# Mixture of experts: weights as whole float32 in column halves, in place of split parts, with a ring of twelve units

## The chip, the cores and the metric

One Trainium2 chip; the kernel runs on one NeuronCore. The metric is device time in microseconds of one execution, median of the runs.

## What is computed

Two network blocks over 256 tokens of width 1024. The first block is a retention and convolution mixer followed by a mixture of 32 experts, the second a gated MLP and a dilated attention. The change is in the experts only:

```
t = u.reshape(256, 1024)
# router: one of 4 groups, the 2 best of its 8 experts, weights -> combine (256 x 32)
for e in range(32):
    h = silu(t @ w_exp_gate[e]) * (t @ w_exp_up[e])          # 1024 x 512 each
    y = y + combine[:, e:e + 1] * (h @ w_exp_down[e])        # 512 x 1024
```

All of it is float32. An expert has three matrices of 2 MB, 32 experts 192 MB: half of what the kernel reads.

## The kernel before

**Units and ring.** Weights arrive in units of 1 MB, 128 partitions x 2048 numbers (`UC` = 4 chunks of 512 columns). An expert has six: gate 0 and 1, up 0 and 1 (each half of the 1024 inputs), down 0 and 1. During the experts the ring has six units of SBUF, one for each part (`SLOT_OF`). The SP queue issues all weight transfers in an order written out by hand (`expert_stream`, L635); each waits until TensorE has finished with the unit that lay in the slot before (`unit_done`).

**Split parts.** TensorE multiplies in the single-pass float32 format `fp32r`, whose operands are rounded. So that nothing is lost, every weight unit is split: ScalarE copies it rounded into `w_hi` (L2767), VectorE subtracts that from the unit and leaves the rest in `w_lo` over the unit itself (L2001; GpSimd does a quarter of the down part, L2373). Each product is made with both parts. Inputs are split as well, into two times 64 columns side by side (`xs`, `hs`): one weight load of 128 columns holds the rounded and the remaining part of 64 gathered tokens, and the two halves of the output are added later by a product with `fold` (L1193).

**One expert (`expert` on each engine, 64 slots of gathered tokens).** On TensorE in this order: two up units (8 chunks x 2 parts = 16 matmuls of 512 columns, L1132 and L1135), the gather of the next expert's tokens (48 bf16 matmuls of 64 columns: `h` in three bf16 parts times the selection `sel`, L1146), the scatter of the expert before (8 matmuls, L1154 and L1156), two transposes of the weighted selection (L1185), the fold (8 products, L1193), the next expert's gate units (16 matmuls), the down units (16 matmuls, L1124). ScalarE also empties PSUM (L2817, L2783), makes the slot weights (L2823), silu (L2825) and the rounded outputs `ye_hi` (L2803); VectorE makes `selT` (L2028), the product of gate and up (L2030), `hs` (L2032), `sel` (L1988) and `selw` (L1994) of experts ahead and `ye_lo` (L2013).

**Around the experts.** The gate units of expert 0 are loaded early into `first_gate`, rounded by ScalarE (L2730) and split by VectorE (L1817) while the mixer ends; up 0, gate 1 and down 0 are loaded into the ring at 531 to 537 us. The router runs from about 542 to 570 us. After expert 31, `scatter_whole` (L1165) adds its output; then VectorE adds the experts to the residual and the second block begins with four units that were loaded ahead (`units_ahead`, L684), the first two rounded by ScalarE (`hi_ahead`, L2798).

**Whole float32 elsewhere.** The ada and tail units of the mixer (`row_unit`, L827) are multiplied unsplit, as float32, in four column quarters of the array (32 columns each); spreads of 128 columns (L843) are float32 too. A float32 matmul stands in the trace as two records, an fp32r or bf16 one as one record.

Of the kernel before, what the change touches and what calls it, by code (L numbers as in the profile page):

```python
# [14 lines left out]
P = 128  # L15
T = 256
# [33 lines left out]
SLOT_OF = {"up": 0, "gate": 2, "down": 4}  # L50
# [48 lines left out]
def build(nc, a, out):  # L99
    with ExitStack() as ctx:  # L100
# [149 lines left out]

        slots_of, fills = [], []
        for n in range(len(units)):
            slots_of.append(n % RING2 if n < n_before else (n - n_before) % RING if n < first["a"] else (n - first["a"]) % RING2)
            fills.append(slots_of.count(slots_of[n]) - (n >= first["a"] and slots_of[n] in (SLOT_OF["gate"], SLOT_OF["gate"] + 1)))


        fills_before = [slots_of[:n_before].count(k) for k in range(RING)]
# [174 lines left out]
        def heads_T(t, tt):  # L432
# [61 lines left out]
        xs = single_pass("xs", KC, P, on=free0 + 3072)  # L494
        sel = nc.alloc_sbuf_tensor_at("sel", [P, NT, SLOTS], BF16, offset=ARENA_AT + 4 * (free0 + 4096))
        selw, _ = carve(NT, 2, SLOTS, on=free0 + 5120)
        selT = single_pass("selT", T, on=free0 + 5376)
        fold, _ = carve(SLOTS, on=free0 + 5632)
        slot_weight, _ = carve(2, on=free0 + 5696)
        weighted, _ = carve(T, on=free0 + 5700)  # L500
        hs = single_pass("hs", FF // P, P, on=free0 + 7424)
        gate_act, _ = carve(T, on=free0 + 7936)
        gate_out, _ = carve(FF, on=free0 + 8192)
        up_out, _ = carve(FF, on=free0 + 8704)
        ye_hi = single_pass("ye_hi", D, on=free0 + 9216)
        ye_lo = single_pass("ye_lo", D, on=free0 + 10240)
        ye, _ = carve(D, on=free0 + 9216)
        w_hi = [single_pass("w_hi_%d" % p, UC, W, on=on) for p, on in enumerate(
            (o_kc, o_vc, o_v, o_v + 2048, o_vc + 2048, o_XT))]
        w_lo = single_pass("w_lo", RING, UC, W)  # L510
# [7 lines left out]
        first_gate = [arena[:, o_:o_ + UC * W].rearrange("p (k c) -> p k c", k=UC) for o_ in (o_qT, o_kT)]  # L518
        first_lo = [single_pass("first_lo%d" % j, UC, W, on=on) for j, on in enumerate((o_qT, o_kT))]
# [27 lines left out]
        def order(kind, e, j, tail=False):  # L547

            return 2 + e * 6 + ({"up": 0, "gate_next": 2, "down": 2 if tail else 4}[kind] + j + 1)
# [6 lines left out]
        def _(sp):  # L556
# [34 lines left out]
            for n in range(n_before):  # L591
# [15 lines left out]
                if n == at_unit["conv", 1, 1]:  # L607

                    sp.wait_ge(S("unit_done"), end_of("ret", 1, 4))
                    for j in range(2):  # L610
                        sp.dma_start(first_gate[j].rearrange("p k c -> p (k c)"), moe_src("gate", 0, j)).then_inc(S("first_full"), 16)
# [2433 lines left out]
```

## Time and profile before

| | before |
|---|---|
| device time, median of 3 runs | 1739.13 us (1737.48 to 1742.75) |
| the profiled execution's own time | 1742.08 us |
| its span | 1740.3 us |
| TensorE busy | 1604.2 us (92%) |
| VectorE busy | 1214.6 us (70%) |
| ScalarE busy | 988.0 us (57%) |
| GpSimd busy | 473.1 us (27%) |
| read from HBM | 378.95 MB, 218 GB/s over the span |

How to read it: the shares are means over stages with different limits. The experts take the stretch from about 575 us (first gate product) to 1146 us (last scatter), a third of the span and more than half of the bytes. The granted TensorE clock is given as a share of full speed.

### The profile page before, as it was taken

Reading aid. Unit: us, or ns where it says so; the run is one execution under the profiler, and the core shown is the slowest. Engines: PE = TensorE matmul, PEld = TensorE weight load, DVE = VectorE, ACT = ScalarE, POOL = GpSimd, SP = SyncE. Lnnn points to the kernel's source line nnn. Section 1 sums busy time; section 2 is a strip of 40 time slices with the busy share of each in tenths; the row PEclk is TensorE's granted clock in tenths of the full one; section 3 lists DMA queues with packets and bytes.
Section 4 is the critical chain, followed back from the end, with each engine's and each line's share of the span. In section 5 each row is a group of like instructions: output and inputs, shape, how many; then the busy total and the mean of one; then the engine's idle time right before and its main releaser. Section 6 shows DMA issues by size and latency. Waiting matters only on the chain.

```text
span 1740.3 us, 23452 instructions
## 1 busy us (share of the span) xinstructions
PE 1604.2 (92%) x8954; PEld 1291.7 (74%) x8954; DVE 1214.6 (70%) x1566; ACT 988.0 (57%) x1081; POOL 473.1 (27%) x132
## 2 busy tenths in 40 slices
PE   5999999999986889999999999969898899999986
PEld 2888888886664677778777878758787687878765
DVE  2688886765347899999999999972611863436793
ACT  2423245543434679898889898835344345464651
POOL 0000000110000031212121212128676476645562
PEclk9999999999996799999999999989999899999997
DMA  8623244246785489999989999837544453433430
GB/s 316 193 99 97 78 142 146 98 156 233 251 294 209 171 351 358 366 367 366 364 348 361 366 373 365 333 108 249 179 152 164 143 170 122 135 130 123 137 118 24
DMA packets 120869, 380.99 MB, mean 219 GB/s; under 512 B 9302, under 2 KB 11134, under 8 KB 96222
## 3 DMA queue, kind: packets, MB, share of 16 engines
q1 hardware_dynamic: 120798, 380.02, 60.0%
q8 instruction: 47, 0.77, 0.2%
q14 instruction: 24, 0.20, 0.0%
HBM read 378.95 MB, written 1.05 MB: 218 GB/s over the span
## 4 chain that ended last, share of the span: by engine, by line
PE 55%; DVE 20%; DMA 10%; issue 8%; ACT 6%; SPq 1%; DVEq 0%; POOL 0%; ACTq 0%; POOLq 0%
PE ps L743 10%; PE ps L744 9%; PE ps L750 9%; DVE w_lo L2001 6%; DMA ring<-in_w_exp_gate 5%; PE ps L908 3%; PE ps L907 3%; PE ps L914 3%; PE ps L1135 2%; PE ps L1132 2%; ACT w_hi L2767 2%; PE ps L807 1%; DVE arena L2263 1%; DVE arena L2265 1%; DMA ring<-in_w_exp_down 1%
## 5 line engine op out<-in xcount | busy, mean ns | idle before, releaser
L2469 ACT ACTIVATE w_hi<-ring 128x2048 fp32r<-128x2048 f32 x130 | 246.9, 1912 | 329.9 <-PE ps L750 141.7
L2001 DVE TENSOR_TENSOR w_lo<-ring,w_hi 128x2048 fp32r<-128x2048 f32 (+1 forms) x190 | 392.2, 2103 | 4.5 <-ACT w_hi L2767 4.5
L2394 POOL TENSOR_TENSOR w_lo<-ring,w_hi 128x2048 fp32r<-128x2048 f32 x71 | 334.1, 4727 | 189.5 <-ACT w_hi L2469 189.5
L2767 ACT ACTIVATE w_hi<-ring 128x2048 fp32r<-128x2048 f32 x190 | 364.9, 1922 | 15.5 <-DMA ring<-in_w_exp_gate 10.1
L2373 POOL TENSOR_TENSOR w_lo<-ring,w_hi 128x1024 fp32r<-128x1024 f32 x32 | 106.4, 3323 | 480.9 <-ACT w_hi L2767 480.9
L743 PE MATMUL ps<-w_hi,xt_hi 128*128 128x512 f32 x512 | 204.5, 399 | 7.2 <-ACT w_hi L2469 4.7
L1460 DVE TENSOR_TENSOR w_lo<-ring,w_hi 128x2048 fp32r<-128x2048 f32 x59 | 134.8, 2287 | 99.4 <-ACT w_hi L2469 99.0
L744 PE MATMUL ps<-w_hi,xt_lo 128*128 128x512 f32 x480 | 189.5, 395 | 0.0
L1132 PE MATMUL ps<-w_hi,xs 128*128 128x512 f32 x512 | 146.3, 408 | 9.0 <-DVE xs L2006 6.9
L743 PE MATMUL ps<-w_hi,yt_hi 128*128 128x512 f32 x352 | 141.1, 401 | 5.8 <-DVE yt_lo L1453 2.8
L1135 PE MATMUL ps<-w_lo,xs 128*128 128x512 f32 x504 | 141.2, 402 | 1.8
L750 PE MATMUL ps<-w_lo,xt_hi 128*128 128x512 f32 x512 | 126.8, 390 | 0.1
L743 PEld LDWEIGHTS ps<-w_hi,xt_hi 128*128 128x128 f32 x512 | 97.7, 191 | 32.6 <-ACT w_hi L2469 5.2
L1132 PEld LDWEIGHTS ps<-w_hi,xs 128*128 128x128 f32 x512 | 95.8, 192 | 32.5 <-issue 7.7
L1135 PEld LDWEIGHTS ps<-w_lo,xs 128*128 128x128 f32 x504 | 91.9, 190 | 35.8 <-DVE w_lo L2001 17.3
L750 PEld LDWEIGHTS ps<-w_lo,xt_hi 128*128 128x128 f32 x512 | 96.1, 188 | 20.6 <-POOL w_lo L2394 0.5
L744 PEld LDWEIGHTS ps<-w_hi,xt_lo 128*128 128x128 f32 x480 | 91.8, 191 | 18.9
L2400 POOL TENSOR_SCALAR arena<-arena 128x4 f32<-128x4 f32 x4 | 8.6, 2152 | 355.7 <-DVE arena L1660 355.7
L1552 DVE SCALAR_TENSOR_TENSOR arena<-arena 128x256 f32<-128x256 f32 x240 | 96.4, 482 | 0.0
L744 PE MATMUL ps<-w_hi,ut_lo_lat 128*128 128x512 f32 x224 | 88.3, 394 | 0.0
L743 PEld LDWEIGHTS ps<-w_hi,yt_hi 128*128 128x128 f32 x352 | 68.0, 193 | 26.7 <-issue 10.7
L750 PE MATMUL ps<-w_lo,yt_hi 128*128 128x512 f32 x352 | 87.1, 389 | 0.0
(330 smaller groups left out, 2904.4 us busy)
## 6 DMA issues: line engine op xcount, KB each, us to landing
ring<-in_w_exp_up SPq DMA_DIRECT2D x64, 1024.0 KB, 8.9
ring<-in_w_exp_down SPq DMA_DIRECT2D x64, 1024.0 KB, 8.0
ring<-in_w_exp_gate SPq DMA_DIRECT2D x62, 1024.0 KB, 6.3
ring<-in_w_in SPq DMA_DIRECT2D x40, 1024.0 KB, 5.1
ring<-in_b_w_in SPq DMA_DIRECT2D x40, 1024.0 KB, 5.1
ring<-in_w_ada SPq DMA_DIRECT2D x24, 1024.0 KB, 6.9
ring<-in_a_w_in SPq DMA_DIRECT2D x24, 1024.0 KB, 6.5
ring<-in_w_ret_out SPq DMA_DIRECT2D x8, 1024.0 KB, 5.4
```

The costliest lines, as they stand in the source:

```text
L743: pe.matmul(o[:, tt, :], hi[:, k, x_], w[:, c, :], start=(bias is None and j == 0 and c == 0), stop=False)
L744: pe.matmul(o[:, tt, :], lo[:, k, x_], w[:, c, :], start=False, stop=False)
L750: mm = pe.matmul(o[:, tt, :], hi[:, (UC * j + c + at) % (UC * nk), x_], w_lo2[:, slots_of[n], c, :], start=False, stop=(j == nk - 1 and c ...
L1132: pe.matmul(ps[:, bank, :], parts(c), w_hi[p][:, c, :], start=(begin and c == 0), stop=False)
L1135: mm = pe.matmul(ps[:, bank, :], parts(c), w_lo[:, p, c, :] if lo is None else lo[:, c, :], start=False, stop=(end and c == UC - 1))
L1460: dve.tensor_tensor(w_lo2[:, slots_of[n]], ring[:, slots_of[n]], w[:, :, :].bitcast(F32), ALU.subtract).then_inc(S("w_lo_vector"), 1)
L1552: ins = dve.scalar_tensor_tensor(conv[:, k, :], z, cwT[:, k, j:j + 1], conv[:, k, :], ALU.mult, ALU.add)
L2001: dve.tensor_tensor(w_lo[:, p, 0:upto], ring[:, p, 0:upto], w_hi[p][:, 0:upto, :].bitcast(F32), ALU.subtract).then_inc(S("lo_ready"), 1)
L2373: pool.tensor_tensor(w_lo[:, p, c:UC], ring[:, p, c:UC], w_hi[p][:, c:UC, :].bitcast(F32), ALU.subtract).then_inc(S("pool_lo"), 1)
L2394: pool.tensor_tensor(w_lo2[:, slots_of[n]], ring[:, slots_of[n]], w[:, :, :].bitcast(F32), ALU.subtract).then_inc(S("w_lo_full"), 1)
L2469: act.activation(part_of(n)[1][:, :, :], ring[:, slots_of[n]], ACT.Copy).then_inc(S("w_hi_full"), 1)
L2767: act.activation(w_hi[p][:, :, :], ring[:, p], ACT.Copy).then_inc(S("hi_ready"), 1)
```

## The change

Expert weights are no longer split. Each unit is multiplied as it lies, as whole float32, with 64 columns of inputs in the array instead of 128: gate and up (`gate_up_product`) run side by side, gate in columns 0 to 63 and up in columns 64 to 127 of the array, each with its own moving weights, and leave in one PSUM bank. The down product does the same with its two output halves. There are no `w_hi`, `w_lo`, `xs`, `hs` and `fold` any more, and no part of GpSimd in the experts. The space of `w_hi` becomes six more ring slots (`homes`), so that two experts' units fit (even experts in `ring`, odd ones in `homes`). Selections and gathers are made for two experts at once: 128 columns a matmul, half of the 1024 features after each expert. One ScalarE copy takes gate and up out of PSUM (`gate_up_left`), four transposes turn them, and the rest of the chain is as before. The scatter uses 64 rows for each output half. Expert 0's units come with the others (`first_pair`). In the last expert ScalarE now does `hi_ahead` for both units before it takes gate and up out.

```diff
-SLOT_OF = {"up": 0, "gate": 2, "down": 4}
+PARTS = [("gate", 0), ("up", 0), ("gate", 1), ("up", 1), ("down", 0), ("down", 1)]
+EVEN_SLOTS = [4, 5, 0, 1, 2, 3]
+ALL_SLOTS = 2 * RING
+        homes = [carve(UC, W, on=on)[0] for on in (o_kc, o_vc, o_vc + 2048, o_XT, o_v, o_v + 2048)]
+            def next_pair(e, rd):
+                for odd in range(2):
+                    for k in range(6):
+                        sp.wait_ge(S("unit_done" + suffix(rd)), e * 6 + (done_base(rd) - 12 + 6 * odd + k + 1))
+                        expert_unit(e, odd, k, rd)
+            def first_pair():
+                sp.wait_ge(S("unit_done"), end_of("mix", 1))
+                for k in range(2):
+                    expert_unit(0, 0, k, 0)
+                sp.wait_ge(S("merged"), 2)
+                for k in (4, 5, 3):
+                    expert_unit(0, 1, k, 0)
+                for k in range(2, 6):
+                    sp.wait_ge(S("unit_done"), max(n for n in range(n_before) if slots_of[n] == expert_slot(0, k)) + 1)
+                    expert_unit(0, 0, k, 0)
+                sp.wait_ge(S("mod_spread"), 8)
+                expert_unit(0, 1, 0, 0)
+                sp.wait_ge(S("eT_turned"), NT)
+                sp.wait_ge(S("h_left"), NT)
+                for k in (1, 2):
+                    expert_unit(0, 1, k, 0)
             def units_ahead(again):
-                    if not again and i < 2:
-                        sp.wait_ge(S("unit_done"), order("up", NE - 1, i) + n_before)
+                    if not again:
+                        sp.wait_ge(S("unit_done"), n_before + 6 * (NE - 2) + EVEN_SLOTS.index(k) + 1)
...
+            def gate_up_product(e, odd, rd):
+                if not odd:
+                    for half in range(2):
+                        pe.wait_ge(S("x_half%d" % half), e + NE * rd + 2)
+                for j in range(2):
+                    for k in (2 * j, 2 * j + 1):
+                        arrived(e, odd, k, rd)
+                    for c in range(UC):
+                        x_ = x_pair[:, UC * j + c, SLOTS * odd:SLOTS * (odd + 1)]
+                        for i in range(2):
+                            mm = pe.matmul(ps[SLOTS * i:SLOTS * (i + 1), 0, :], x_, weights(odd, 2 * j + i)[:, c, :],
+                                           start=(j == 0 and c == 0), stop=(j == 1 and c == UC - 1))
+                            if c == UC - 1:
+                                mm.then_inc(S("unit_done" + suffix(rd)), 1)
+            def down_product(e, odd, rd):
+                for j in range(2):
+                    arrived(e, odd, 4 + j, rd)
                     for r in range(2):
                         for half in range(2):
+                            mm = pe.matmul(ps[SLOTS * half:SLOTS * (half + 1), 3, :], hT[:, 2 * j + r, :], weights(odd, 4 + j)[:, 2 * r + half, :],
+                                           start=(j == 0 and r == 0), stop=(j == 1 and r == 1))
+                    mm.then_inc(S("unit_done" + suffix(rd)), 1)
+            def gather(e, half, rd):
+                pe.wait_ge(S("sel_ready"), e + NE * rd + 2)
+                for k in range(UC * half, UC * (half + 1)):
+                    o_ = P * (k % UC)
                     for i, part in enumerate(h_parts):
                         for tt in range(NT):
+                            mm = pe.matmul(ps[:, 0 if half else 2, o_:o_ + P], part[:, tt, P * k:P * (k + 1)], sel[:, tt, :],
             def scatter(begin):
                 for tt in range(NT):
+                    for part in (ye_hi, ye_lo):
+                        for j in range(2):
+                            s_ = slice(SLOTS * j, SLOTS * (j + 1))
+                            mm = pe.matmul(y[tt][:, j, :], selT[s_, P * tt:P * (tt + 1)], part[s_, :],
...
 # TensorE, expert(e, odd): gate_up_product, scatter, 2 transposes of selw,
+                pe.wait_ge(S("gate_up_left"), gi + 1)
+                for c in range(FF // P):
+                    mm = pe.transpose(ps[:, 1, P * c:P * (c + 1)], gate_up_out[:, P * c:P * (c + 1)], ident)
+                if not tail:
+                    gather(e + 2, odd, rd)
                 pe.wait_ge(S("selT"), gi + 1)
                 pe.wait_ge(S("slot_weight"), gi + 1)
+                pe.wait_ge(S("hT_ready"), gi + 1)
+                down_product(e, odd, rd)
...
-            for j in range(2):
-                dve.wait_ge(S("hi_ready"), 1 + j)
-                dve.tensor_tensor(first_lo[j][:, :, :], first_gate[j], w_hi[...].bitcast(F32), ALU.subtract)
+            def second_half(e, rd):
+                dve.wait_ge(S("gathered"), e + NE * rd + 2)
+                dve.tensor_copy(x_pair[:, UC:KC, :].rearrange("p k s -> p (k s)"), ps[:, 0, :]).then_inc(S("x_half1"), 2)
...
             # ScalarE
-            act.wait_ge(S("first_full"), 32)
-            for j in range(2):
-                act.activation(w_hi[SLOT_OF["gate"] + j][:, :, :], first_gate[j], ACT.Copy)
+            def expert(e, odd, rd, head=False, ahead=False):
                 if not head:
+                    act.wait_ge(S("unit_done" + suffix(rd)), done)
+                    act.activation(ye_hi[:, :], ps[:, 3, :], ACT.Copy, scale=slot_weight[:, 0:1]).then_inc(S("ye_hi"), 1)
+                if ahead:
+                    act.wait_ge(S("unit_done" + suffix(rd)), done + 2)
+                    for j in range(AHEAD):
+                        hi_ahead(j, False)
+                act.wait_ge(S("unit_done" + suffix(rd)), done + 4)
+                act.activation(rows_by_pair(gate_up_out), pairs_of(ps[:, 0, :]), ACT.Copy).then_inc(S("gate_up_left"), 1)
```

## Rows read from the trace of the kernel before

**Rows 1.** page part 2, forty slices: DMA share in tenths, and GB/s moved
```profile
DMA  8623244246785489999989999837544453433430
GB/s 316 193 99 97 78 142 146 98 156 233 251 294 209 171 351 358 366 367 366 364 348 361 366 373 365 333 108 249 179 152 164 143 170 122 135 130 123 137 118 24
```

**Rows 2.** windows: stretch, length, busy us (instructions), granted clock, DMA share, GB/s
```profile
608.00:622.00 14.00, 9.15 (x36) 6.80 (x36) 12.76 (x11) 8.03 (x10) 7.16 (x3) 0.96 1.01 421
660.00:1100.00 440.00, 433.22 (x3135) 347.38 (x3133) 423.69 (x406) 395.66 (x383) 85.47 (x26) 1.00 0.93 365
```

**Rows 3.** waits of the SP queue, 660 to 1100: total us, times, longest
```profile
SPq L635 <- PE ps L1135: 278.4, 101, 7.7
```

**Rows 4.** tile ring on SP, 660 to 1100: issue to landing
```profile
DMA to landing us min/median/max: 4.7/8.0/9.8
```

**Rows 5.** groups by line, 660 to 1100: busy us, mean ns, idle before
```profile
L2001 DVE TENSOR_TENSOR w_lo<-ring,w_hi 128x2048 fp32r<-128x2048 f32 x128 | 287.9, 2280 | 0.0
...
L2817 ACT ACTIVATE arena<-ps 128x512 f32<-128x512 f32 x26 | 29.0, 1115 | 0.0
...
L2030 DVE TENSOR_TENSOR ps<-ps,arena 128x256 f32<-128x256 f32 x25 | 10.6, 422 | 0.0
...
L2825 ACT ACTIVATE arena<-ps 128x256 f32<-128x256 f32 x26 | 10.3, 395 | 0.0
```

**Rows 6.** timeline of TensorE, one expert: start, us, line, out<-in, count
```profile
800.36 0.47 PE L1154 MATMUL ps<-ye_hi,selT 128*128 128x512 f32 x1
...
802.29 0.38 PE L1185 MATMUL ps<-arena 128*128 128x128 f32 x2
802.50 1.90 PE L1193 MATMUL ps<-arena 128*128 128x64 f32 x16
804.31 1.19 PE L1132 MATMUL ps<-w_hi,xs 128*128 128x512 f32 x4
...
816.00 1.57 PE L1146 MATMUL ps<-sel,h_part 128*128 128x64 bf16 x48
817.41 0.47 PE L1154 MATMUL ps<-ye_hi,selT 128*128 128x512 f32 x1
```

**Rows 7.** timeline of TensorE where whole float32 units run in column quarters
```profile
441.39 1.02 PE L843 MATMUL ps<-arena 128*128 128x512 f32 x2
442.33 1.06 PE L827 MATMUL ps<-ring,arena 128*32 128x512 f32 x8
443.33 0.50 PE L743 MATMUL ps<-w_hi,yt_hi 128*128 128x512 f32 x1
...
456.83 1.92 PE L827 MATMUL ps<-ring,arena 128*32 128x512 f32 x16
```

**Rows 8.** line L827: instructions, ns min/median/max
```profile
L827 PEld LDWEIGHTS ps<-ring,arena x192: 106/109/156, 14.5 to 535.0; 128*32 128x32 f32 x192
```

**Rows 9.** groups by line, TensorE, 256 float32 columns: 64 rows, 128 rows
```profile
L976 PE MATMUL ps<-arena 128*128 128x256 f32 x64 | 16.4, 379 | 0.0
L1285 PE MATMUL ps<-arena 64*128 64x256 f32 x96 | 15.9, 389 | 0.0
```

**Rows 10.** timeline of TensorE, first expert
```profile
570.68 2.72 PE L1146 MATMUL ps<-sel,h_part 128*128 128x64 bf16 x48 [3.87 <-DVE sel L1988]
...
575.32 2.07 PE L1132 MATMUL ps<-w_hi,xs 128*128 128x512 f32 x4 [1.71 <-DVE arena L1965]
...
580.29 1.09 PE L1135 MATMUL ps<-first_lo,xs 128*128 128x512 f32 x4
```

**Rows 11.** timeline of VectorE and ScalarE ahead of the router
```profile
526.56 4.49 DVE L1817 TENSOR_TENSOR first_lo<-arena,w_hi 128x2048 fp32r<-128x2048 f32 x2
...
542.22 4.76 ACT L2740 ACTIVATE h_part<-arena 128x1024 bf16<-128x1024 f32 x1
```

**Rows 12.** timeline of TensorE, last expert's down product and scatter
```profile
1135.06 2.04 PE L1124 MATMUL ps<-w_hi,hs 128*128 128x512 f32 x4 [3.61 <-DVE hs L2032]
...
1144.27 1.98 PE L1165 MATMUL ps<-arena,selT 128*128 128x512 f32 x4 [0.39 <-ACT arena L2788]
```

More of the change, by code:

```diff
@@ L545, in done_base, with full_of, filled_times, weights @@
             return PER_ROUND * (rd - 1) if rd else n_before
-        def order(kind, e, j, tail=False):
-            return 2 + e * 6 + ({"up": 0, "gate_next": 2, "down": 2 if tail else 4}[kind] + j + 1)
+        def full_of(s_, rd):
+            return S("w_full%d%s" % (s_, suffix(rd) if s_ < RING2 else ""))
+        def filled_times(s_, rd):
+            return NE // 2 * (rd - 1) if rd and s_ < RING2 else fills_before[s_] + NE // 2 * rd
+        def weights(odd, k):
+            s_ = expert_slot(odd, k)
+            return ring[:, s_] if s_ < RING else homes[s_ - RING]
         MOE_NORM = H // 2 + 2
@@ L1169, in expert @@
-            def expert(e, rd, head, tail, begin):
-                gi = e + NE * rd
-                for j in range(2):
-                    stacked_product(1, xs_part(j), SLOT_OF["up"] + j, order("up", e, j), rd, j == 0, j == 1)
-                if not tail:
-                    pe.wait_ge(S("sel_ready"), gi + 2)
-                    pe.wait_ge(S("gate_left"), gi + 1)
-                    gather()
+            def expert(e, odd, rd, head=False, begin=False, tail=False):
+                gi = e + (odd + NE * rd)
+                gate_up_product(e, odd, rd)
@@ L1208, in experts @@
+                gather(0, 1, rd)
                 if rd == 0:
                     most_filled()
[L1210 to L1216 removed]
@@ L1217, in experts @@
-                expert(NE - 1, rd, False, True, False)
+                expert(0, 0, rd, head=True)
+                expert(0, 1, rd, begin=(rd == 0))
+                with pe.Fori(2, NE - 3, 2) as e:
+                    for odd in range(2):
+                        expert(e, odd, rd)
+                for odd in range(2):
+                    expert(NE - 2, odd, rd, tail=True)
                 scatter_whole(rd)
@@ L2047, in experts @@
+                if not (odd and tail):
+                    select_weights(e + (odd + 1), rd)
+                if odd and not tail:
+                    second_half(e + 2, rd)
             def experts(rd):
@@ L2849, in _ @@
+            def experts(rd):
+                first_half(0, rd)
+                expert(0, 0, rd, head=True)
+                expert(0, 1, rd)
+                first_half(2, rd)
+                with act.Fori(2, NE - 3, 2) as e:
+                    for odd in range(2):
+                        expert(e, odd, rd)
+                    first_half(e + 2, rd)
+                expert(NE - 2, 0, rd)
+                expert(NE - 2, 1, rd, ahead=(rd == 0))
+                output_whole(rd)
             experts(0)
```

326 lines of the change are left out of this document (83 added, 243 removed).

## Prediction

> **What bounds the kernel now.** I read the forty slices first: across the experts (slices 14 to 25) the DMA queues are nine tenths busy and move about 365 GB/s, the highest of the kernel [rows 1]. So the weight stream looks like the limit. Two views say it isn't quite. The windows show that over 440 us the share is 0.93 at 365 GB/s, but that in 14 us in which transfers were queued behind each other the engines moved 421 GB/s at share 1.01 [rows 2]. And SP, which issues them, waited 278.4 us in those 440 for TensorE to give up a slot (line L1135 alone) [rows 3]: with six units of ring the stream runs out of places. TensorE's timeline gives the period of one expert, from scatter to scatter 817.41 - 800.36 = 17.05 us [rows 6]. TensorE and VectorE fill it: TensorE is busy 433.22 and VectorE 423.69 of 440 us [rows 2], most of VectorE's in remainders of 2.28 us each, without idle before them [rows 5]. So three limits lie close together: work on TensorE 16.8 us (17.05 x 433.22 / 440), VectorE 16.4, and the stream, 6.29 MB an expert, 14.9 us at 421 GB/s. A change that takes work from both engines gains until the stream is met.
>
> **VectorE, ScalarE, GpSimd.** All remainders go, and all rounding copies of weights. What is left on VectorE is at most ten instructions of 0.4 to 0.8 us (like L2030, 422 ns), on ScalarE the copy of gate and up (1.115 us, like L2817), silu (0.395, like L2825) and three or four more [rows 5]: under 6 us of each in an expert. They count only where TensorE waits for them.
>
> **TensorE, one expert.** Prices at full clock:
> - Gate and up: 8 chunks x 2 halves, whole float32. The nearest row is L827, the same form in column quarters. Eight records (one unit) take 1.06 us, sixteen 1.92 us [rows 7]; so each set of four records side by side costs (1.92 - 1.06) / 2 = 0.43 us, no more than one record of L843 alone (two in 0.94 us with the change of form behind them [rows 7]). A pair of halves then is two records deep, 0.86 us. 8 x 0.86 = 6.9 us. If halves did not run side by side it would be 13.8; I take 6.9, since quarters do.
> - Down: 4 pairs, 3.4 us.
> - Gather: 24 matmuls of 128 columns. Now 48 of 64 columns take 817.41 - 816.00 = 1.41 us, 29 ns each [rows 6], of which 64 / 2.4 = 27 ns are columns; 128 columns give 56 ns, 24 x 0.056 = 1.3 us. It was 1.4.
> - Scatter: 8 matmuls on 64 rows. Now 802.29 - 800.36 = 1.93 us [rows 6]. Row halves on different rows overlap: 256 columns on 64 rows cost 15.9 / 96 = 0.166 us a record, on 128 rows 16.4 / 64 = 0.256 [rows 9]. By that 1.93 x 0.65 = 1.25; bounds 0.97 and 1.93.
> - Transposes: 2 take 0.21 us [rows 6], so 2 + 4 take 0.6. The folds, 804.31 - 802.50 = 1.81 us [rows 6], go.
> - Changes of array form: L843 to L827 0.94 - 0.86 = 0.08 us, L827 to the next 1.00 - 0.86 = 0.14 us [rows 7]. Four an expert, 0.4 us. Bounds 0 and 1.
> Sum 6.9 + 3.4 + 1.3 + 1.25 + 0.6 + 0.4 = 13.9 us, against about 16.8 now.
> - The chain between gate/up and down is not prefetched any more as the gate half was: last record (0.6) + copy 1.1 + transposes 0.4 (and 0.2 for their end) + silu 0.4 + product 0.4 + some 0.4 of signals = 3.5 us. Beside it TensorE has scatter, transposes and gather, 3.6 us with the changes of form. So it is just hidden; if not, 0 to 1 us more. I take 13.9, range 13.6 to 15.5.
>
> **The stream.** 6.29 MB at 421 GB/s is 14.9 us, more than 13.9. So TensorE now waits for the stream, and the twelve slots keep it fed: SP issues unit n + 12 when unit n is done, so even across the 3.6 us gap and a down product some six transfers are queued, 15 us of work. The stream then decides, as one length:
> 1. The 12 units of experts 0 and 1 are loaded while the router runs, when the queues are nearly idle (slice 13 moves 171 GB/s [rows 1]). They cost nothing on the path, since the router ends at 570 us.
> 2. Start of gate/up of expert 0, now 575.32 [rows 10]. Both halves of the gather come first: 48 x 128 columns at the 1.2 GHz level, 2 x 2.72 [rows 10] = 5.4 us instead of 2.7; the remainder of `xs` and a wait fall away. Two more selections 0.4. I take 577.2, +1.9. The 4.49 us of first remainders on VectorE stand before the norm; but ScalarE comes to the router's input at 542.22 straight from other work (its line shows no idle) [rows 11], so they give nothing. Bounds 0 and 4.
> 3. The first slots come free after 4 pairs of expert 0; half of them run at the lower clock, as the first products do now (2.07 us for four against 1.09 later [rows 10]): 5 us, 582.2. From issue to landing one unit takes at least 4.7 us [rows 4], of which 2.5 are its own bytes at 421 GB/s: 2.2 of delay, 584.4.
> 4. 180 units of 1.0486 MB and 1.5 MB of gains are 190.3 MB: 452 us at 421 GB/s. Last unit at 1036.4.
> 5. The tail. In the last expert ScalarE is to round two units of the second block before it takes gate and up out of PSUM, and these lie behind expert 31's in the queue: 2 x 2.7 us, rounding 1.9, copy 1.1, transposes, silu and product 2.1, down at the lower clock 6.9 (it is now at that level after an idle of 3.61 us: 2.04 us for four [rows 12]), output 1.1, last scatter 3.7 (8 float32 matmuls, two by two). Sum 22.2: 1058.6. Bounds 10 (if the stream is ahead) and 24.
> The experts now end at 1144.27 + 1.98 = 1146.25 [rows 12]. So the change gives 1146.25 - 1058.6 = 87.6 us. What follows is the same work with the same four units ahead. From the profiled 1742.08 us that is 1654.5; this execution lies 2.95 us above the median of the runs, 1739.13, so I predict 1739.1 - 87.6 = 1651.5 us. Could TensorE be the limit? 577.2 + 4 for the cold start + 32 x 13.9 ends before the last unit lands; up to about 14.6 us an expert the stream decides.
>
> **Rivals.**
> - A, the forecast: side by side, stream at 410 to 430 GB/s, 1636 to 1665 us.
> - B, the same but the long stream holds less than the 14 us did. The 440 us give 365 / 0.93 = 392 GB/s at a full share [rows 2]; 190.3 MB then take 485 us, 33 more: 1685. TensorE at 15.5 us an expert would give a similar time: 577 + 4 + 496 + 10 = 1087, 1680.
> - C, weight loads are not hidden in this form. 24 records' depth an expert x 0.109 us for a load [rows 8] = 2.6 us, TensorE 16.5: 577 + 4 + 528 + 8 = 1117, 1710. Against it: in L827 a set of records follows the last after 0.43 us with its loads in between. The Trainium skill (TensorE: Matmul & The Clock Gate, Part 3, "What overlaps and what doesn't") has a rule that weight loads overlap running matmuls only where the row group differs; here both halves use all rows. The trace disagrees for quarters, no row shows it for halves.
> - D, 365 GB/s is already what a long stream gets. 190.3 MB take 521 us: 1127.6, a gain of 18.6, 1720. For it: eleven slices in a row (14 to 24) lie at 348 to 373 [rows 1]. Against it: SP's waits and the 421. The Trainium skill (DMA: Bandwidth & Descriptors, the table at its head) puts a core's HBM share at about 358 GB/s; by its number the gain would be 8 us, 1731, an estimate. The trace went above it.
> - E, slower: the two column halves run one after the other, because they read the same inputs and write the same bank. Gate/up 13.8, down 6.9, an expert 24.2 us: 577 + 4 + 774 + 8 = 1363, plus 217: 1956. The change turns slower once TensorE needs more than (1146 - 589) / 32 = 17.4 us an expert. Against it: quarters write one bank side by side [rows 7].
> - F, TensorE's clock falls to 1.2 GHz because it waits more. At that level it would need 28 us and no longer wait; now it comes up within 5 us of steady work [rows 10]. Twelve units of ring cover such dips. It adds some us to A, and no case of its own.
>
> **How the numbers follow.** A 0.62, B 0.20 (1665 to 1700), C 0.05, D 0.06, E 0.05, and 0.02 for a gain beyond A. The likeliest is A: 1651.5. The range, 1630 to 1702, takes in A and B with the bounds of the tail (-12, +2), the start (-4) and the rate. About 0.3%, 5 us, can be told from no change. Faster 0.93, same 0.02, slower 0.05.
>
> **What would show it.** Steps in the changed profile: the share of DMA at 1.0 with about 420 GB/s in the slices of the experts; waits of TensorE for landings of `ring` and `homes`; a period of about 14.9 us; pairs of whole float32 records 0.43 us apart; SP waiting seldom long; the first gate/up near 577, the last scatter near 1059, with ScalarE's gate/up copy of expert 31 behind two roundings. Records 0.86 us apart would mean E, 0.54 C, a full share at 365 GB/s D. The prediction is wrong if the stream falls below 400 GB/s or TensorE never waits for it.

## The result and the profile after

| | before | after |
|---|---|---|
| device time, median | 1738.93 us | 1645.87 us (1645.51 to 1650.64, 4 runs) |
| ratio, 95% interval | | 0.9468 [0.9445, 0.9491] |
| the profiled execution's own time | 1742.08 us | 1645.66 us |
| its span | 1740.3 us | 1643.9 us |
| experts end (last scatter) | 1146.25 us | 1050.52 us |
| TensorE, VectorE, ScalarE, GpSimd busy | 1604, 1215, 988, 473 us | 1494, 764, 582, 367 us |

1651.5 us was predicted. Before has four runs here; the three ahead of the prediction gave 1739.13. The median fell by 93.1 us; in the profiled executions the experts end 95.7 us earlier.

Page part 2 of the kernel after, the slices of [rows 1]: the share of the DMA queues and GB/s.

```profile
DMA  8632235344876699999999999365446344433330
GB/s 311 204 128 77 78 102 181 104 132 154 308 280 230 261 405 422 422 422 422 421 422 422 422 422 422 113 227 189 144 152 205 129 138 144 130 127 129 129 116 26
```

Counted from 0, slices 15 to 24 stand at 421 or 422 GB/s, where those of before had 348 to 373. The windows say the same for 400 us within the experts (stretch and length, then busy us of TensorE, its weight loads, VectorE, ScalarE and GpSimd, granted clock, DMA share, GB/s); SP's waits for slots, to be held against [rows 3], follow:

```profile
600.00:1000.00 400.00, 380.80 (x2352) 166.60 (x2350) 73.45 (x205) 76.68 (x149) 4.75 (x2) 1.00 1.01 422
```

```profile
SPq L638 <- PE ps L1140: 165.8, 56, 3.7
SPq L638 <- PE ps L1151: 134.6, 54, 4.1
```

VectorE and ScalarE are busy 73 and 77 of 400 us, where they had 424 and 396 of 440. SP still waits for slots, but now it does so with a full queue behind it. Page part 6 gives the median from issue to landing of a gate unit:

```profile
ring<-in_w_exp_gate SPq DMA_DIRECT2D x32, 1024.0 KB, 23.0
```

All ring units of before had 8.0 us [rows 4] (gate units alone 6.3). At 2.5 us a unit, 23.0 us is about nine units of bytes, an estimate of how many share the queue. TensorE's timeline, one expert, answers to [rows 6]:

```profile
802.52 3.65 PE L1140 MATMUL ps<-ring,arena 128*64 128x512 f32 x16 [1.12 <-DMA ring<-in_w_exp_up]
806.10 0.50 PE L1172 MATMUL ps<-ye_hi,selT 64*128 64x512 f32 x2
806.44 0.40 PE L1172 MATMUL ps<-ye_lo,selT 64*128 64x512 f32 x2
...
807.23 0.44 PE L1197 MATMUL ps<-arena 128*128 128x128 f32 x2
807.51 0.60 PE L1202 MATMUL ps<-arena 128*128 128x128 f32 x4
807.94 1.50 PE L1162 MATMUL ps<-sel,h_part 128*128 128x128 bf16 x24
809.38 3.65 PE L1151 MATMUL ps<-ring,arena 128*64 128x512 f32 x16
812.86 3.60 PE L1140 MATMUL ps<-arena 128*64 128x512 f32 x16
817.28 3.65 PE L1140 MATMUL ps<-arena 128*64 128x512 f32 x16 [0.82 <-DMA arena<-in_w_exp_up]
820.87 0.50 PE L1172 MATMUL ps<-ye_hi,selT 64*128 64x512 f32 x2
```

This period is 820.87 - 806.10 = 14.77 us; it alternates with 15.0. TensorE lives on the twelve units that were loaded ahead at first: the first eight periods, from the scatter at 592.01 to that at 701.78, are 13.7 us each, without a wait for a landing. From 716.47 to 1029.63 the stream sets them: 21 periods of 14.91 us on average, what 6.29 MB take at 422 GB/s. 16 records of a pair of halves take 3.65 us, that is eight steps of two records, 0.43 us apart; in front of the second half of gate and up TensorE waits about 1 us for a landing. Start and end of the experts, on TensorE:

```profile
565.96 4.25 PE L1162 MATMUL ps<-sel,h_part 128*128 128x128 bf16 x48 [4.20 <-DVE sel L1989]
...
571.39 7.09 PE L1140 MATMUL ps<-ring,arena 128*64 128x512 f32 x32 [1.08 <-DVE arena L1965]
...
1039.21 1.12 PE L1202 MATMUL ps<-arena 128*128 128x128 f32 x4 [8.02 <-ACT arena L2753]
1041.46 6.29 PE L1151 MATMUL ps<-arena 128*64 128x512 f32 x16 [1.13 <-DVE arena L2018]
1048.53 1.99 PE L1182 MATMUL ps<-arena,selT 64*128 64x512 f32 x8 [0.78 <-ACT arena L2729]
```

and on ScalarE in the last expert, where two units of the second block are rounded (L2739) before gate and up leave PSUM (L2753):

```profile
1033.67 1.91 ACT L2739 ACTIVATE w_hi_ahead<-ring 128x2048 fp32r<-128x2048 f32 x1 [11.43 <-DMA ring<-in_a_w_in]
1036.29 1.91 ACT L2739 ACTIVATE w_hi_ahead<-ring 128x2048 fp32r<-128x2048 f32 x1 [0.71 <-DMA ring<-in_a_w_in]
1038.11 1.05 ACT L2753 ACTIVATE arena<-ps 128x512 f32<-128x512 f32 x1
```

### The profile page after: what moved, and what is told of

The parts are those of the page before. It is cut to its first block, busy times and chain, and to the rows that moved or that the text cites. A ratio compares the mean times of both kernels' runs of the same rounds, so it can differ in the third digit from the quotient of the medians.

```text
span 1643.9 us, 19822 instructions
## 1 busy us (share of the span) xinstructions
PE 1493.9 (91%) x7802; PEld 1043.1 (63%) x7802; DVE 763.6 (46%) x1294; ACT 581.7 (35%) x777; POOL 367.2 (22%) x100
## 4 chain that ended last, share of the span: by engine, by line
PE 61%; DMA 21%; DVE 11%; ACT 3%; issue 2%; SPq 1%; POOL 0%; DVEq 0%; POOLq 0%; ACTq 0%
DMA ring<-in_w_exp_up 17%; PE ps L752 11%; PE ps L753 10%; PE ps L759 10%; PE ps L1140 6%; PE ps L917 3%; PE ps L916 3%; PE ps L923 3%; PE ps L1151 2%; DMA ring<-in_a_w_in 2%; PE ps L816 2%; DVE arena L2232 1%; DVE arena L2234 1%; DMA ring<-in_w_ada 1%; DVE arena L1391 1%
## 5 line engine op out<-in xcount | busy, mean ns | idle before, releaser
L2425 ACT ACTIVATE w_hi<-ring 128x2048 fp32r<-128x2048 f32 x130 | 246.9, 1911 | 322.3 <-PE ps L759 142.0
L2016 DVE TENSOR_SCALAR selT<-ps 128x256 fp32r<-128x256 f32 x32 | 13.6, 425 | 256.0 <-ACT arena L2755 256.0
L1140 PE MATMUL ps<-ring,arena 128*64 128x512 f32 x512 | 115.1, 594 | 12.5 <-DMA ring<-in_w_exp_up 11.4
L1140 PE MATMUL ps<-arena 128*64 128x512 f32 x512 | 115.0, 594 | 9.9 <-DMA arena<-in_w_exp_up 9.9
L2753 ACT ACTIVATE arena<-ps 128x512 f32<-128x512 f32 x32 | 35.0, 1093 | 219.7 <-PE ps L1140 219.7
L2352 POOL TENSOR_TENSOR w_lo<-ring,w_hi_ahead 128x2048 fp32r<-128x2048 f32 x1 | 4.5, 4517 | 417.5 <-ACT w_hi_ahead L2739 417.5
L1140 PEld LDWEIGHTS ps<-ring,arena 128*64 128x64 f32 x512 | 37.2, 137 | 87.2 <-issue 85.9
L1140 PEld LDWEIGHTS ps<-arena 128*64 128x64 f32 x512 | 38.3, 137 | 83.9 <-issue 83.7
```

Source lines behind the costliest of these rows:

```text
L1140: mm = pe.matmul(ps[SLOTS * i:SLOTS * (i + 1), 0, :], x_, weights(odd, 2 * j + i)[:, c, :], start=(j == 0 and c == 0), stop=(j == 1 and c ...
L2352: pool.tensor_tensor(w_lo2[:, slots_of[n]], ring[:, slots_of[n]], w[:, :, :].bitcast(F32), ALU.subtract).then_inc(S("w_lo_full"), 1)
L2425: act.activation(part_of(n)[1][:, :, :], ring[:, slots_of[n]], ACT.Copy).then_inc(S("w_hi_full"), 1)
L2753: act.activation(rows_by_pair(gate_up_out), pairs_of(ps[:, 0, :]), ACT.Copy).then_inc(S("gate_up_left"), 1)
```

## The experiments

All ratios are against the kernel before, run on the same chip. The runs come from several chips, on which before took 1738.0 to 1741.9 us, so small differences between two runs are told by their ratios, not by their times alone.

| run | time, us | ratio |
|---|---|---|
| after | 1645.87 | 0.9468 [0.9445, 0.9491] |
| e1_halves_in_turn | 1674.65 | one run |
| e2_half_bytes | 1610.89 | 0.9251 [0.9225, 0.9277] |
| e3_six_ahead | 1662.47 | 0.9551 [0.9521, 0.9580] |
| e4_round_after | 1638.92 | 0.9416 [0.9392, 0.9439] |
| e5_gate_loads_back | 1650.97 | 0.9497 [0.9482, 0.9512] |
| e6_gains_first | 1642.89 | 0.9441 [0.9424, 0.9458] |
| e7_both | 1634.42 | 0.9408 [0.9390, 0.9425] |
| e8_one_half | 1829.36 | 1.0523 [1.0493, 1.0553] |
| b2_half_remainders | 1747.90 | 1.0062 [1.0041, 1.0084] |
| b4_half_rounding | 1736.13 | 0.9983 [0.9968, 0.9998] |
| b5_half_gate_up_bytes | 1699.91 | 0.9752 [0.9726, 0.9778] |

### Is the stream the limit of the kernel after?

**e2_half_bytes**: from expert 2 on, only half of each unit's bytes is loaded.

```diff
+            def expert_unit(e, odd, k, rd, part=slice(0, UC * W)):
...
-                        expert_unit(e, odd, k, rd)
+                        expert_unit(e, odd, k, rd, slice(0, UC * W // 2))
```

> From expert 2 on only the first half of every weight unit is transferred; the rest of a slot keeps what lay there, so half of the weights of these experts are wrong. All matmuls stay. Theory: the stream sets the time of the changed kernel. Then the period falls from 14.77 us to TensorE's own, 13.7 us as the first expert shows, the last scatter comes at about 571 + 32 x 13.7 + 9 = 1018 and the kernel takes about 1613 us (33 less). Rival: the chain and TensorE already need 14.7 us and the waits for the stream are only where slack collects; then it stays at 1640 to 1646.

1610.89 us, as the theory had it (1613). The windows of e2, and the first scatter records of two experts in a row:

```profile
600.00:800.00 200.00, 200.00 (x1244) 87.25 (x1242) 39.30 (x110) 40.56 (x79) 4.78 (x2) 1.00 0.73 237
```

```profile
799.81 0.50 PE L1172 MATMUL ps<-ye_hi,selT 64*128 64x512 f32 x2
...
813.53 0.49 PE L1172 MATMUL ps<-ye_hi,selT 64*128 64x512 f32 x2
```

TensorE is busy without a gap and the queues are not full. The period is 813.53 - 799.81 = 13.72 us, in every expert to the last but one: what the work on TensorE takes by itself. So the stream costs 14.91 - 13.72 = 1.2 us in each of the last 22 experts of after, 26 us from the first scatter to the last, and the rest behind the last unit: from the last expert's first scatter to the end of the experts after takes 20.9 us, e2 9.6. Against these 37 us, e2's gather started 2.1 us later. In the medians 35.0 us are left.

**e3_six_ahead**: SP waits for six units more before each, so that six units are ahead in place of twelve.

```diff
-                        sp.wait_ge(S("unit_done" + suffix(rd)), e * 6 + (done_base(rd) - 12 + 6 * odd + k + 1))
+                        sp.wait_ge(S("unit_done" + suffix(rd)), e * 6 + (done_base(rd) - 6 + 6 * odd + k + 1))
```

> Transfers are issued when unit n - 6 is done instead of n - 12: the ring is in effect six units deep again, as before the change, with everything else changed. Theory 1: what the twelve units bring is only the loading of two experts ahead of the first; at 13.7 us of TensorE an expert six units keep the queue filled nearly all the time, and the kernel takes 1646 to 1660 us. Theory 2: the deep ring is what fills the queue; with six the engines run dry in the gap between gate/up and down as they did before, at about 365 to 392 GB/s (16 to 17.2 us an expert), and the kernel takes 1685 to 1725 us.

1662.47 us, 16.6 more than after: near theory 1 (1646 to 1660), far from theory 2. The windows of e3:

```profile
600.00:1000.00 400.00, 371.60 (x2272) 161.26 (x2270) 73.66 (x200) 74.68 (x144) 4.69 (x2) 1.00 1.01 421
```

The rate is that of after. Twelve slots are not what brings 422 GB/s: six ahead do in this kernel. That this is because nothing is rounded or split any more between landing and product is argued: no run puts only that back. The loss lies at the start. SP's first issue for expert 2, in after and in e3:

```profile
575.04 0.33 SPq L638 DMA_DIRECT2D ring<-in_w_exp_gate  x1
```

```profile
591.23 0.33 SPq L638 DMA_DIRECT2D ring<-in_w_exp_gate  x1
```

The stream starts again 16.2 us later; 1.6 us of that are this execution's later gather, 14.6 the edit. TensorE pays them at once, in periods of 15.47 and 19.60 us for the next experts, and then runs at 14.9 us as in after.

### Do the halves run side by side?

**e1_halves_in_turn**: the four gate chunks of a unit pair are issued, then the four up chunks.

```diff
-                    for c in range(UC):
-                        x_ = x_pair[:, UC * j + c, SLOTS * odd:SLOTS * (odd + 1)]
-                        for i in range(2):
+                    for i in range(2):
+                        for c in range(UC):
+                            x_ = x_pair[:, UC * j + c, SLOTS * odd:SLOTS * (odd + 1)]
```

> The gate and up matmuls are no longer issued alternately: four chunks of gate in one column half, then four of up in the other; nothing else changes. Theory: TensorE keeps the order of issue and only neighbours on different columns overlap. Then a unit pair needs about 6.5 us instead of 3.45, an expert 20 us instead of 13.7, TensorE sets the time and not the stream, and the kernel takes about 571 + 32 x 20 + 9 + 595 = 1815 to 1825 us, slower than before the change. Rival: TensorE finds the other half by itself, records stay 0.43 us apart in pairs, and the time stays at 1646.

1674.65 us, which neither theory had. TensorE's timeline of e1:

```profile
811.99 8.92 PE L1140 MATMUL ps<-arena 128*64 128x512 f32 x32
```

8.92 us in place of 7.0, and a period of 15.60 us with TensorE never idle in 600 to 1000 us. The single records start 0.43 us apart: four alone, then 24 in twelve pairs, then four alone, 20 steps x 0.43 = 8.6 us where 16 would do. Before the record that ends the first gate unit (it alone signals `unit_done`, and seven gate records precede it) ten others have started, so three of them are up records that come later in the program. TensorE took the other column half's products up to two chunks (of two records each) before their turn. The first theory had no such look-ahead, the rival set no bound to it. It is a single run, and its gather starts at 571.63 us, 5.7 us later than in after and ahead of anything that e1 changes; the price of the order is therefore read from the 8.92 us and not from the time.

**e8_one_half**: gate and up both in columns 0 to 63.

```diff
-                            mm = pe.matmul(ps[SLOTS * i:SLOTS * (i + 1), 0, :], x_, weights(odd, 2 * j + i)[:, c, :],
-                                           start=(j == 0 and c == 0), stop=(j == 1 and c == UC - 1))
+                            mm = pe.matmul(ps[0:SLOTS, 0, :], x_, weights(odd, 2 * j + i)[:, c, :],
+                                           start=(j == 0 and c == 0 and i == 0), stop=(j == 1 and c == UC - 1 and i == 1))
```

> The kernel after with gate and up both in columns 0 to 63 of the array and in one accumulation (so that sum of both stands in place of the gate product, and the up product is not made: the output is another). Bytes, count of matmuls, their order, copies and gathers are those of after. It prices the rival that halves run one after another. If only different column halves overlap, gate and up take 16 x 2 x 0.43 = 13.8 us in place of 6.9, an expert 13.7 + 6.9 = 20.6 us: 571 + 32 x 20.6 + 9 + 595 = about 1835 us, at some 305 GB/s. If TensorE overlaps any two float32 products that stand next to each other, the period stays at 14.8 to 15.6 us and the time at 1646 to 1675 us.

1829.36 us, as the first reading had it. TensorE's timeline of e8, one expert:

```profile
812.97 0.50 PE L1172 MATMUL ps<-ye_hi,selT 64*128 64x512 f32 x2
...
819.72 13.90 PE L1140 MATMUL ps<-ring,arena 128*64 128x512 f32 x32
833.55 0.50 PE L1172 MATMUL ps<-ye_hi,selT 64*128 64x512 f32 x2
```

Period 20.58 us, gate and up 13.90. Products in the same columns don't overlap here; in different halves they do. That the halves lie in different columns is worth 183.5 us, about twice what the whole change gains. One thing isn't separated: e8 also puts both products in one accumulation, so the same columns with two places in PSUM stay untested.

### Where the start and the tail go

**e5_gate_loads_back**: the kernel after loads expert 0's gate units into `arena` at the old place as well, and nobody uses them.

```diff
+                if n == at_unit["conv", 1, 1]:
+                    sp.wait_ge(S("unit_done"), end_of("ret", 1, 4))
+                    for j, o_ in enumerate((o_qT, o_kT)):
+                        sp.dma_start(arena[:, o_:o_ + UC * W], moe_src("gate", 0, j)).then_inc(S("first_full"), 16)
```

> The changed kernel with the two early 1 MB transfers of the first gate units put back where the kernel before had them (behind the bias rows at 480 us); nobody uses what they bring. Theory: these two stood in the queue ahead of the conv and mix units, and the router started 3.5 of its 5 us earlier because they are gone (the other 1.5 us came at 407 us, where the two kernels are the same). Then the first gate/up product comes 3 to 4 us later and the kernel takes 1649 to 1650 us. Rival: the 5 us came from the remainders that VectorE no longer makes ahead of the norm; then this kernel stays at 1646.

1650.97 us, 5.1 more than after; the two intervals still touch (0.9482 against 0.9491), so the trace has to decide. TensorE's timeline of e5:

```profile
570.55 5.28 PE L1167 MATMUL ps<-sel,h_part 128*128 128x128 bf16 x48 [4.20 <-DVE sel L1994]
...
577.02 3.23 PE L1145 MATMUL ps<-ring,arena 128*64 128x512 f32 x14 [0.99 <-DVE arena L1970]
```

The gather starts 4.6 us later than in after (570.55 against 565.96). By itself that would say little: in the eight executions without the two transfers it starts anywhere from 565.5 to 571.6 us, but most of that spread is there before (SP's issue behind the place of the transfers stands at 480.6 to 485.2). What the transfers do is seen in ScalarE's wait for the mixer's next unit, in before, after and e5:

```profile
ACT w_hi L2469 <- DMA ring<-in_w_mix_out: 8.3, 1, 8.3
```

```profile
ACT w_hi L2425 <- DMA ring<-in_w_mix_out: 3.6, 1, 3.6
```

```profile
ACT w_hi L2430 <- DMA ring<-in_w_mix_out: 8.5, 1, 8.5
```

The five traces with the transfers have 8.3 to 8.7 us there, the eight without 3.2 to 3.6. From SP's first issue of that part of the mixer (487.74 in e5) to the gather it is 81.1 to 84.4 us with and 77.7 to 79.4 without. So two transfers of 1 MB delay the mixer's last units and the router by 3 to 5 us. The gather takes 5.28 us in e5 in place of 4.25, at a granted clock of 0.50 against 0.65; that is not theirs, since e6 and e7 have 5.28 us without them. The removed work of VectorE and ScalarE isn't back in e5.

**e4_round_after**: ScalarE takes gate and up of the last expert out first and rounds the second block's two units after that.

```diff
-                if ahead:
-                    act.wait_ge(S("unit_done" + suffix(rd)), done + 2)
-                    for j in range(AHEAD):
-                        hi_ahead(j, False)
 ...
                 act.activation(...ACT.Silu).then_inc(S("gate_act"), 1)
+                if ahead:
+                    for j in range(AHEAD):
+                        hi_ahead(j, False)
```

> In the last expert ScalarE rounds the two units of the second block after the silu instead of before it takes gate and up out of PSUM. Theory: in the changed kernel the last expert waits 8.0 us for that copy, which waits for two transfers behind the last weights, and its down product then runs at the lower clock. Both go: 8 to 10 us less, 1636 to 1638 us. Rival: the second block needs these units just as early, so that the wait only moves there: 0 to 3 us less.

1638.92 us, 6.9 less than after by the medians and 9.0 by the ratios (0.9416 against 0.9468). TensorE's timeline of e4, last expert:

```profile
1032.22 3.65 PE L1151 MATMUL ps<-arena 128*64 128x512 f32 x16 [1.13 <-DVE arena L2018]
1038.34 2.42 PE L1182 MATMUL ps<-arena,selT 64*128 64x512 f32 x8 [2.47 <-ACT arena L2729]
```

The wait of 8.02 us before L1202 is gone, and the down product takes 3.65 us in place of 6.29. From the last expert's first scatter to the end it is 11.7 us in place of 20.9.

**e6_gains_first**: the gains of norm 2 are loaded before expert 2's units, not behind them.

```diff
-                next_pair(2, rd)
 ...
                         sp.dma_start(v, a[name][0:1].broadcast_to([P, D])).then_inc(S("load_gains"), 16)
+                next_pair(2, rd)
```

> The three gain rows (1.5 MB) are transferred before the stream of expert 2 on, while the queues are idle, instead of twelve units later. Theory: the stream is one full queue and everything in it costs its bytes: 1.57 MB at 422 GB/s, 3.7 us less, 1642 us. Rival: the tail or TensorE covers it: no change, 1646.

1642.89 us, 3.0 less, in the direction expected; the intervals of e6 and after overlap, so the times alone don't show it. The traces do: from the start of the first gather to the end of the experts e6 takes 1047.70 - 567.11 = 480.6 us, after 1050.52 - 565.96 = 484.6, 4.0 us less where 3.7 were expected (e5, with the gains in their old place, has the same 484.6).

**e7_both**: e4 and e6 together.

> Both edits at once, rounding after the silu and gains ahead of the stream: they lie at different ends of the stream, so they should add up: 1638.9 - 3.7 = 1635 us. If they overlap, 1639.

1634.42 us, the lowest median: 11.4 us under after and 104 under before. That the two add up is what the traces say (1038.20 - 565.69 = 472.5 us from gather to the end of the experts, 12.1 less than after); the interval of e7 overlaps that of e4 alone.

### What held the kernel before?

**b2_half_remainders**: the kernel before, with remainders made and multiplied for chunks 0 and 1 of gate and up units only.

```diff
-                for c in range(UC):
+                for c in range(UC // 2):
                     mm = pe.matmul(ps[:, bank, :], parts(c), w_lo[:, p, c, :] if lo is None else lo[:, c, :], start=False, ...)
...
-                        remainder(SLOT_OF["gate"] + j, order("gate_next", e, j), rd)
+                        remainder(SLOT_OF["gate"] + j, order("gate_next", e, j), rd, UC // 2)
...
-                        remainder(SLOT_OF["up"] + j, order("up", e + 1, j), rd)
+                        remainder(SLOT_OF["up"] + j, order("up", e + 1, j), rd, UC // 2)
...
```

> The kernel before, with the remainder of gate and up units made and multiplied for two of their four chunks only (so half of that correction is missing): VectorE has 4.6 us less and TensorE 1.85 us less in each expert, transfers and ring are the same. Theory: the engines set the period of 17.05 us, not the stream. Then it falls to about 15.2 to 15.4 us and the kernel takes 1740 - 32 x 1.7 = about 1685 us. Rival: six slots and the way units are held limit the stream at 365 to 370 GB/s; then little changes, 1730 to 1740 us.

1747.90 us: no gain at all, but 0.6% more. Windows of b2, to be held against [rows 2]:

```profile
660.00:1100.00 440.00, 389.98 (x2860) 316.82 (x2859) 317.62 (x401) 391.09 (x377) 81.93 (x25) 0.98 0.92 359
```

TensorE lost 43 us of its 433 and VectorE 106 of 424, and the period did not fall: over this stretch 17.5 us on average, where before has 17.3 (its expert at 800 us took 17.05). ScalarE was as busy as before, so the next run relieves it as well.

**b4_half_rounding**: b2, and ScalarE rounds only these chunks.

```diff
-                    pe.matmul(ps[:, bank, :], parts(c), w_hi[p][:, c, :], start=(begin and c == 0), stop=False)
+                    pe.matmul(ps[:, bank, :], parts(c), w_hi[p][:, c % 2, :], start=(begin and c == 0), stop=False)
...
-                act.activation(w_hi[p][:, :, :], ring[:, p], ACT.Copy).then_inc(S("hi_ready"), 1)
+                n_ = UC if kind == "down" else UC // 2
+                act.activation(w_hi[p][:, 0:n_, :], ring[:, p, 0:n_], ACT.Copy).then_inc(S("hi_ready"), 1)
```

> The kernel before with half of its gate and up remainders as in b2_half_remainders, and now also with half of ScalarE's rounding of these units: ScalarE rounds chunks 0 and 1 of a gate or up unit, and TensorE multiplies each of the two twice in place of four different ones (part of the computation is left out: chunks 2 and 3 of all gate and up weights but those of expert 0's gate). TensorE's work is that of b2, ScalarE loses 4 x 0.95 = 3.8 us an expert, VectorE nothing. Theory 1, ScalarE's list in fixed order closed the period of b2 (391.09 of 440 us busy, six roundings of 1.92 us an expert and the waits around them): TensorE's 15.4 us an expert come to decide, the period falls from 17.35 to 15.4 to 16, and the time from 1747.9 to about 1690 (1680 to 1710), with 390 GB/s or more. Theory 2, the ring of six units with its exchange (a slot comes free, then 4.7 to 8 us until the next unit has landed) closes it whatever the engines do: the period stays at 17.0 to 17.4 and the time at 1735 to 1750.

1736.13 us. Theory 1 fell. Windows of b4, then ScalarE's timeline (the rounding of down 0 and the next inputs) and TensorE's gate products of two experts:

```profile
660.00:1100.00 440.00, 392.93 (x2896) 320.54 (x2897) 325.71 (x414) 321.12 (x386) 80.10 (x26) 0.98 0.93 366
```

```profile
812.38 1.91 ACT L2768 ACTIVATE w_hi<-ring 128x2048 fp32r<-128x2048 f32 x1 [0.40 <-DMA ring<-in_w_exp_down]
814.20 0.58 ACT L2773 ACTIVATE xs<-ps 128x512 fp32r<-128x512 f32 x1
```

```profile
798.49 1.19 PE L1132 MATMUL ps<-w_hi,xs 128*128 128x512 f32 x4 [1.55 <-DVE xs L2006]
...
802.34 1.19 PE L1124 MATMUL ps<-w_hi,hs 128*128 128x512 f32 x4 [0.80 <-DVE hs L2032]
...
815.64 1.20 PE L1132 MATMUL ps<-w_hi,xs 128*128 128x512 f32 x4 [1.30 <-DVE xs L2006]
```

No engine is full, the queues stand at 0.93, and the period is 17.15 us here (17.2 on average). This is a ring of waits: the down products (802.34) free down 0's slot at about 804.3, SP issues the next unit at 804.48, it lands at 812.38 behind its neighbours, ScalarE rounds it, and only then, next in its list, makes the inputs on which the next gate products wait. The landing leg alone is 7.9 us of the 17.15.

**b5_half_gate_up_bytes**: b4, and the unused halves of the gate and up units aren't loaded.

```diff
-                sp.dma_start(ring[:, k].rearrange("p k c -> p (k c)"), moe_src(kind, e, j)).then_inc(...)
+                h_ = slice(0, UC * W if kind == "down" else UC * W // 2)
+                sp.dma_start(ring[:, k].rearrange("p k c -> p (k c)")[:, h_], moe_src(kind, e, j)[:, h_]).then_inc(...)
```

> b4_half_rounding with half of the bytes of each gate and up unit in the stream (chunks 2 and 3, which b4 doesn't use, aren't loaded any more; the same part of the computation is left out as in b4). 4.19 MB an expert in place of 6.29; engines' work and the order of all lists are those of b4. In b4 the loop of an expert runs through landings: down 0 issued at 804.48 when its slot came free, landed at 812.38, rounded by ScalarE, and only behind that in ScalarE's list the next inputs, and then the gate products at 815.64. Theory 2 of b4 (the exchange of the six slots closes the period): a transfer of half a unit takes 1.2 us less, and those queued ahead of a down unit too, so down units land 2 us or more sooner, and the period falls from 17.15 towards TensorE's 15.3 us: 15.3 to 16.0, 1736 - 31 x (17.15 - 15.6) = 1688 us (1675 to 1705). Rival, the fixed order of the engines' lists closes it and landings don't: the period stays at 17.0 to 17.2 and the time at 1725 to 1740.

1699.91 us: 36 less than b4, with the same work on all engines. Windows of b5, landing of its `ring` units over 660 to 1040 us, and one period on TensorE:

```profile
660.00:1040.00 380.00, 356.01 (x2690) 290.74 (x2689) 298.13 (x382) 290.35 (x358) 68.59 (x24) 1.00 0.75 260
```

```profile
DMA to landing us min/median/max: 3.6/7.0/8.7
```

```profile
801.47 0.48 PE L1155 MATMUL ps<-ye_hi,selT 128*128 128x512 f32 x1
...
817.04 0.48 PE L1155 MATMUL ps<-ye_hi,selT 128*128 128x512 f32 x1
```

Landings come 1.3 us sooner (b4's median was 8.3 us). The period shown is 15.57 us; the average from 671.30 to 1072.35 is 16.0, where b4 has 17.2, and 31 times the difference is the 36 us. Only bytes differ between b4 and b5, so the landings, with the exchange of six slots, close the period of b4. Before is less clear-cut. Taking half of the gate and up work off its engines gains nothing (b2, b4), so their work is not what holds it; but TensorE is busy for 433.22 of 440 us there, so fewer bytes alone, which no run tried, could gain only 0.3 us of 17.3 (an estimate). It takes both.

## Why the prediction was right, step by step

- **What bounds before.** The prediction saw SP's waits and called the ring short of places, but then set three limits side by side, two of them engines' work, and left ScalarE (396 of 440 us) out. b2 and b4 show that taking work from TensorE and VectorE alone, or from ScalarE too, gains next to nothing there (ratios 1.0062 and 0.9983). Only the gate and up part was relieved, and by half. The sentence "a change that takes work from both engines gains until the stream is met" was wrong as a general rule. That it came out right here is in part luck: the change does something else along with it, which the prediction did not count, since a unit is multiplied as it lands and its slot is busy for a shorter time. e3, at the full rate even with six ahead, fits this but does not single it out.
- **TensorE, 13.9 us predicted, 13.72 measured (e2).** Gate and up 6.96 (6.9), down 3.49 (3.4), gather 1.43 (1.3), transposes 0.71 (0.6), scatter with the change of form behind it 1.13 (1.25 without). The price of halves, read from column quarters, was the decisive step, and it held to 1%.
- **The chain between gate/up and down is just hidden.** L1151 waits twice in 416 records of 660 to 1100 us, 1.13 us each time, in experts 30 and 31, which have no gather beside the chain. In the others it doesn't wait. Right.
- **Who waits for whom.** "TensorE now waits for the stream" holds from expert 10 on (counted from 0), at 14.91 us a period, as predicted (14.9). Until then it runs at its own 13.72 us on what was loaded ahead. The time is the same by either reading, since the stream is one length from 577 us on.
- **The rate.** 421 GB/s from 14 us of before, 422 over 400 us of after. Right; rival B, that a long stream holds only 392, and rival D, 365, fall. The Trainium skill (HBM Reference, Specifications) says that a core streaming alone measures about 425 GB/s against a share of about 358 when both cores of a pair stream; one core ran here, and the 422 agree with the first number.
- **Weight loads (rival C).** The steps are 0.43 us apart with 137 ns loads between them (mean, L1140), so they are hidden. The rule of the Trainium skill that the prediction weighed (TensorE: Matmul & The Clock Gate, Part 3, "What overlaps and what doesn't") isn't what this trace shows for column halves.
- **Start.** 577.2 predicted, 571.39 measured. The 5.8 us have three parts. The two transfers of `first_gate` that the change removes give 3.2 us between these two executions (81.1 and 77.9 us from the mixer's issue to the gather) and 4.9 against e5. The prediction asked what their remainders on VectorE cost (nothing, which e5 bears out: without them it takes 82.8 us from the mixer's issue to the gather, where the executions that have them take 81.1 to 84.4) and not what their bytes cost, though they stood ahead of the mixer's last units in SP's queue. That is the step that was missed. Another 1.6 us had already been gained at SP's issue at 413.22 in before and 411.56 in after, where both kernels do the same; both times occur in variants of either, so it was luck. The last 1.1 us are the gather and what follows it, part of which ran above the lower clock. The term lies outside its bounds of 0 and 4 us on a delay: it went below nothing, to -3.9.
- **First slots.** 3.65 us after the first product (SP issues at 575.04) and not 5: the first expert's 32 records take 7.09 us, all at full clock. The gather before them had brought it up.
- **Bytes.** From 577.2 (575.04 and 2.2 of delay) to about 1031.2 (the first unit of the second block landed at 1033.67, 2.5 us for its bytes before it): 454 us, where 452 were predicted.
- **Tail.** 22.2 us predicted, 1050.52 - 1031.2 = 19.3 measured. The mechanism was right: 8.02 us of idle before L1202, behind two roundings, and e4 takes it away (6.9 us by the medians, 9.0 by the ratios). The last scatter was mis-sized: 1.99 us, not 3.7, since its 64-row halves overlap too.
- **The sum.** The experts' end was predicted at 1058.6 and came at 1050.52: 5.8 from the start, 1.4 from the first slots, 2.9 from the tail, less 2 from the stream. Of the 8.1 us, 5.6 show in the median. 1.6 of them are the luck named above.
- **Rival E, slower.** Its mechanism exists: e8, with gate and up in the same columns, is 5% slower than before. Its price for gate and up was right (13.90 us against 13.8 predicted); down products one after another were not tried. e1 shows that even a less favourable order of issue keeps most of the overlap.

## What to carry to other kernels

When all engines are nearly full beside a stream at nine tenths, ask how long one slot is held from issue to release; shortening that may gain where relief of the engines gains nothing (b4 against b5). Whole float32 products of 64 columns, two side by side, cost as much as one here (0.43 us for two records), and need no splitting on other engines. And count what a removed transfer did to those queued behind it.

## What was not expected of the hardware

- TensorE starts products of another column half ahead of three records of this half that were issued before them: e1, 8.92 us where one record at a time would give 13.8.
- 421 or 422 GB/s were held in ten slices in a row, within 1 GB/s, with medians of 23 to 25 us from issue to landing of a weight unit.
- In b4 a period of 17.15 us stood with no engine above 90% and the queues at 0.93: a loop of landings and in-order lists looks almost like a bandwidth limit in the shares.
